# Order of the late experts in a two-layer mixture-of-experts step, and of the first products

## The reference

```python
def _hyena_filter(L, ...):                      # taps of the long convolution
    h = sin(f_freq * (feat @ f_w1 + f_b1))
    h = sin(f_freq * (h @ f_w2 + f_b2))
    return (h @ f_w3) * exp(-t * abs(decay))

def _adaln(cond, w, b):                         # w: 1024 x 6144 for each layer
    return split(silu(cond) @ w + b, 6)

def _hier_moe(x, ...):                          # for each layer
    g_sel = argmax(t @ w_group + b_group)       # one of 4 groups
    top_w, top_i = top_k(softmax(e_logits of that group), 2)
    for e in range(16):
        a, b = split(t @ w_up[e], 2)            # 1024 -> 2 x 512
        y += combine[:, e] * ((silu(a) * b) @ w_down[e])   # 512 -> 1024
```

## Time and profile before

| | us |
|---|---|
| Median of 3 runs | 1127.4 (1126.07 to 1128.08) |
| The profiled execution, its own time | 1126.63 |
| Its span in the profile | 1124.8 |
| TensorE busy | 1033.4 (92% of the span) |
| VectorE busy | 598.1 (53%) |
| ScalarE busy | 211.4 (19%) |
| GpSimd busy | 181.9 (16%) |
| Chain that ended last: TensorE | 73% of the span |
| Chain that ended last: DMA | 9% |
| Mean rate of DMA over the span | 296 GB/s |

### The profile page before, as it was taken

One profiled execution on the slowest core, in us unless ns is written; L12 is line 12 of the kernel. 1 busy time (PEld: TensorE's weight loads), 2 busy tenths in 40 slices (PEclk: granted clock), 3 DMA queues, 4 the chain that ended last, 5 costly groups with the idle time before them and its releaser, 6 DMA issues.

```text
span 1124.8 us, 26238 instructions
## 1 busy us (share of the span) xinstructions
PE 1033.4 (92%) x10516; PEld 619.3 (55%) x10516; DVE 598.1 (53%) x1404; ACT 211.4 (19%) x501; POOL 181.9 (16%) x217
## 2 busy tenths in 40 slices
PE   6999999899887999999969999999988999999773
PEld 2545555385554666666645554575455666665442
DVE  5437898745552333333389991585573333333226
ACT  4242323002310001000050000462231010000002
POOL 1200000410121222222200000254013222222112
PEclk9999999999998999999989999699989999999997
DMA  9994477940679999999987787942097998999991
GB/s 336 403 377 147 179 254 295 398 172 1 264 305 389 392 388 388 388 382 390 386 337 262 262 326 268 320 120 76 2 366 277 353 388 297 385 385 388 393 358 61
DMA packets 114954, 333.43 MB, mean 296 GB/s; under 512 B 11681, under 2 KB 24417, under 8 KB 114497
## 3 DMA queue, kind: packets, MB, share of 16 engines
q1 hardware_dynamic: 91858, 299.65, 70.4%
q0 software_dynamic: 6224, 23.05, 5.8%
q10 hardware_dynamic: 16800, 9.72, 3.1%
HBM read 323.47 MB, written 20.45 MB: 306 GB/s over the span
## 4 chain that ended last, share of the span: by engine, by line
PE 73%; DMA 9%; DVE 8%; SPq 4%; ACT 2%; issue 2%; POOL 1%; POOLq 0%; DVEq 0%; ACTq 0%
PE bank L733 71%; DMA ring<-in_moe_w_down 5%; SPq L491 3%; DMA ring<-in_moe_w_up 2%; POOL P L707 1%; PE bank L1176 1%; DVE st L1954 1%; DVE P L2012 1%; DMA bm<-in_na_bias 1%; DVE hT L1733 1%; DMA row_beta<-in_ln_b 1%; ACT x L1347 1%; DMA slots<-tok,idx_i 0%; PE bank L937 0%; DVE x L1759 0%
## 5 line engine op out<-in xcount | busy, mean ns | idle before, releaser
L733 PE MATMUL bank<-ring,xgT 128*32 128x256 f32 x4224 | 247.3, 386 | 15.2 <-DMA ring<-in_moe_w_up 14.7
L733 PE MATMUL bank<-hT,ring 128*128 128x384 f32 x640 | 207.2, 486 | 2.1 <-DVE hT L1733 2.1
L733 PEld LDWEIGHTS bank<-ring,xgT 128*32 128x32 f32 x4224 | 146.5, 111 | 97.5 <-issue 13.6
L1919 DVE TENSOR_TENSOR he<-sa,bank 128x128 f32<-128x128 f32 x66 | 19.0, 288 | 318.6 <-ACT sa L1405 318.6
L733 PEld LDWEIGHTS bank<-hT,ring 128*128 128x128 f32 x640 | 121.4, 190 | 87.5 <-issue 3.8
L685 POOL TENSOR_TENSOR yg<-ysb,gate_s 128x256 f32<-128x256 f32 x128 | 90.8, 730 | 388.6 <-ACT ysb L1410 388.6
L1555 DVE CUSTOM_DVE_ANT_0 ring<-ring,ring 128x1024 f32<-128x1024 f32 x120 | 146.9, 1224 | 4.6 <-PE bank L733 1.0
L733 PE MATMUL bank<-ring,heT 128*32 128x256 f32 x2112 | 129.7, 386 | 7.3 <-DMA ring<-in_moe_w_down 7.3
L733 PE MATMUL bank<-yg,ohT 32*128 32x256 f32 x1632 | 108.3, 394 | 2.9 <-DVE yg L1948 2.9
L733 PEld LDWEIGHTS bank<-ring,heT 128*32 128x32 f32 x2112 | 63.3, 110 | 63.2 <-issue 30.1
L733 PEld LDWEIGHTS bank<-yg,ohT 32*128 32x128 f32 x1632 | 75.3, 186 | 36.6 <-issue 27.4
(11 more groups left out here) (272 smaller groups left out, 1040.6 us busy)
## 6 DMA issues: line engine op xcount, KB each, us to landing
ring<-in_moe_w_up SPq DMA_DIRECT2D x64, 2048.0 KB, 23.7
ring<-in_moe_w_down SPq DMA_DIRECT2D x32, 2048.0 KB, 19.8
ring<-in_k_ada SPq DMA_DIRECT2D x15, 2048.0 KB, 10.3
ring<-in_w_ada SPq DMA_DIRECT2D x9, 2048.0 KB, 13.1
ring<-in_na_w_qkv SPq DMA_DIRECT2D x6, 2048.0 KB, 13.4
slots<-in_k_zero POOLq DMA_DIRECT2D x2, 5632.0 KB, 26.1
ring<-in_hy_w_in SPq DMA_DIRECT2D x5, 2048.0 KB, 12.9
group_row<-slots ACTq DMA_DIRECT2D x264, 32.0 KB, 5.2
```

The costliest lines, as they stand in the source:

```text
L733: return nc.tensor.matmul(out, lhsT, rhs, start=first, stop=last)
L1919: v.tensor_tensor(he[:], sa[:], ps[0][:, 128:256], ALU.mult).then_inc(S["he_ready"], 1)
```

## The change

Two parts.

**Order of the late experts.** The key that turns a rank into a place has a slope of 3 on one side of its top and of 1.5 on the other, where both slopes were 2 before. Rank r gets the smaller of 3r - 11.75 and -(3r - 11.75)/2, and the places go by that number: of the ranking's many end one is taken, then two of its few end. The table `MC_ORDER`, which holds the sorted keys, is changed alike.

**Beginning.** `mlp1` stands before the last two decay products. ScalarE does both sines first, then the exponentials, and its copies of modulation rows and sums are placed between them one by one. TensorE computes the rows of `cond0` before the taps, and then in turn: taps of a tile, sum of a piece, rows of the next piece. The piece pair `cond2` is now `cond2` and `cond3`; what was `cond3` to `cond7` is `cond4` to `cond8`, in the same places. VectorE copies two quarters of the decay row after each argument reduction, where it copied four after the first.

```diff
-for _name, _n in [("mlp0", 1), ("decay", 4), ("mlp1", 1), ("filt0", 4), ("cond0", 2), ("filt1", 4), ("cond1", 2), ("filt2", 4), ("cond2", 4),
-                  ("xm0", 8),
+for _name, _n in [("mlp0", 1), ("decay0", 1), ("decay1", 1), ("mlp1", 1), ("decay2", 1), ("decay3", 1),
+                  ("cond0", 1), ("filt0", 4), ("cond0_sum", 1), ("cond1", 1), ("filt1", 4), ("cond1_sum", 1),
+                  ("cond2", 1), ("filt2", 4), ("cond2_sum", 1), ("cond3", 1), ("cond3_sum", 1), ("xm0", 8),
...
+ORDER_SHIFT = 11.75
...
-    moe[:, MC_ORDER:MC_ORDER + EXPERTS] = np.arange(EXPERTS) - (EXPERTS - 0.5)
+    slope = 3.0 * np.arange(EXPERTS - FIRST) - ORDER_SHIFT
+    moe[:, MC_ORDER:MC_ORDER + EXPERTS] = np.concatenate([np.arange(FIRST) - 20.0, np.sort(np.minimum(slope, -0.5 * slope))])
...
-            for c in range(4):
-                mm(bank(G_AT["decay"] + c)[:, :], ones[:], dabs[0:1, 512 * c:512 * c + 512]).then_inc(group_ready, 1)
-            pe.wait_ge(mh_ready, 1)
-            mm(bank(G_AT["mlp1"])[:, 0:TOK], fw2, mh1[:]).then_inc(group_ready, 1)
-            pe.wait_ge(first_in, 16)
-            pe.wait_ge(scond_ready, 1)
-            pe.wait_ge(cond_sum_ready, 1)
-            pe.wait_ge(mh_ready, 2)
-            pe.wait_ge(filt_in, 32)
-            for t in range(TT):
...
-                cond(*COND_SEG[t])
+            spread_decay(0)
+            spread_decay(1)
+            pe.wait_ge(mh_ready, 1)
+            mm(bank(G_AT["mlp1"])[:, 0:TOK], fw2, mh1[:]).then_inc(group_ready, 1)
+            spread_decay(2)
+            spread_decay(3)
+            pe.wait_ge(first_in, 16)
+            pe.wait_ge(scond_ready, 1)
+            pe.wait_ge(cond_sum_ready, 1)
+            cond_rows_of(0)
+            pe.wait_ge(mh_ready, 2)
+            pe.wait_ge(filt_in, 32)
+            for t in range(TT):
+                filter_taps(t)
+                cond_sum_of(t)
+                cond_rows_of(t + 1)
+            cond_sum_of(3)
...
-            for c in range(4):
-                wait_evacuated(act, G_AT["decay"] + c)
-            decays(0)
             act.wait_ge(marg_ready, 2)
             nc.scalar.activation(mh2[:], marg[:], ACT.Sin).then_inc(mh_ready, 1)
+            for c in range(4):
+                wait_evacuated(act, G_AT[f"decay{c}"])
+            decays(0)
+            cond_rows_copied(0)
             decays(1)
-            cond(*COND_SEG[0])
+            cond_sum_copied(0)
             decays(2)
-            cond(*COND_SEG[1])
-            cond(*COND_SEG[2])
+            cond_rows_copied(1)
+            cond_sum_copied(1)
+            cond_rows_copied(2)
+            cond_sum_copied(2)
+            cond_rows_copied(3)
+            cond_sum_copied(3)
...
-                if n == 0:
-                    for c in range(4):
-                        g = G_AT["decay"] + c
-                        wait_group(dve, g)
-                        v.tensor_copy(dabs[:, 512 * c:512 * c + 512], ps[bank_of(g)][:, :]).then_inc(evacuated[g % 8], 1)
+                for c in (2 * n, 2 * n + 1):
+                    g = G_AT[f"decay{c}"]
+                    wait_group(dve, g)
+                    v.tensor_copy(dabs[:, 512 * c:512 * c + 512], ps[bank_of(g)][:, :]).then_inc(evacuated[g % 8], 1)
...
-                link(v.tensor_scalar(order_rank[:, FIRST:], order_rank[:, FIRST:], 2.0, 0.5 - late, ALU.mult, ALU.add))
+                link(v.tensor_scalar(order_rank[:, FIRST:], order_rank[:, FIRST:], 3.0, -ORDER_SHIFT, ALU.mult, ALU.add))
...
-                link(v.scalar_tensor_tensor(out=order_at[:, FIRST:], in0=order_rank[:, FIRST:], scalar=-1.0, in1=order_rank[:, FIRST:],
+                link(v.scalar_tensor_tensor(out=order_at[:, FIRST:], in0=order_rank[:, FIRST:], scalar=-0.5, in1=order_rank[:, FIRST:],
```

More of the change, by code:

```diff
@@ L106, in bank_of @@
     return (g + shift) % 8
-def ada_row(n):
-    return 0 if n == 0 else 2 * n - 1
-def ada_col(n, count):
-    return min(2 * n + 2, 2 * count - 1)
 V_ADA, V_CC, V_CS, V_BQK = 0, 96, 104, 112
@@ L439, in last_group @@
             def last_group(j):
-                for seg, _, _, count in COND_SEG:
-                    if 0 <= j - W_AT[seg] < count:
-                        return G_AT[seg] + ada_row(j - W_AT[seg])
+                for seg, _, _ in COND_SEG:
+                    if j == W_AT[seg]:
+                        return G_AT[seg]
                 for l in range(DEPTH):
@@ L541, in cond @@
             def cond(k):
-                seg, l, n0, count = COND_SEG[k]
-                for n in range(count):
-                    load(W_AT[seg] + n, A["w_ada"][l][:, (n0 + n) * 512:(n0 + n + 1) * 512], 8)
+                seg, l, n = COND_SEG[k]
+                load(W_AT[seg], A["w_ada"][l][:, n * 512:(n + 1) * 512], 8)
             def load_named(name):
@@ L584, in _ @@
                     sp.dma_start(dft[:], A["k_dft"]).then_inc(dft_in, 16)
-                    sp.wait_ge(group_ready, G_AT["decay"] + 4)
+                    sp.wait_ge(group_ready, G_AT["decay3"] + 1)
                     sp.dma_start(skip[:], bass.AP(A["hy_d"].tensor, A["hy_d"].offset, [[0, 128], [1, D]])).then_inc(dft_in, 16)
@@ L733, in mm @@
                 return nc.tensor.matmul(out, lhsT, rhs, start=first, stop=last)
-            def cond(name, l, n0, count):
-                for n in range(count + 1):
-                    if n < count:
-                        i = W_AT[name] + n
-                        out = bank(G_AT[name] + ada_row(n))
-                        wait_weights(pe, i)
-                        w = w_view(i, 8, 512)
-                        for k in range(KT):
-                            q = slice(32 * (k % 4), 32 * (k % 4) + 32)
-                            last = mm(out[q, :], scond[:, k, :], w[:, k, :], k < 4, k >= 4)
-                        last.then_inc(group_ready, 1)
-                    if n >= 1:
-                        out = bank(G_AT[name] + ada_col(n - 1, count))
-                        wait_evacuated(pe, G_AT[name] + ada_row(n - 1))
-                        for f in range(4):
-                            last = mm(out[:, 2 * f:2 * f + 2],
-                                      arow_at[l][:, (n0 + n - 1) % 2, f * 128:(f + 1) * 128], cond_sum[:])
-                        last.then_inc(group_ready, 1)
             def cond_rows_of(k):
-                name, l, n0, _ = COND_SEG[k]
+                name, l, n0 = COND_SEG[k]
                 i = W_AT[name]
@@ L896, in _ @@
                 if n in (1, 3):
[L897 removed]
+                    cond_rows_of(6 + n // 2)
                 elif n == 2:
[L899 removed]
+                    cond_sum_of(6)
                 elif n == 4:
[L901 to L903 removed]
+                    cond_sum_of(7)
+                    cond_rows_of(8)
+            cond_sum_of(8)
             pe.wait_ge(Y_ready, 3)
@@ L1325, in _ @@
                                      ).then_inc(evacuated[g % 8], 1)
-            cond_sum_copied(4)
-            for k in (5, 6, 7):
+            cond_sum_copied(5)
+            for k in (6, 7, 8):
                 cond_rows_copied(k)
```

61 lines of the change are left out of this document (23 added, 38 removed).

## The result

| | before | change |
|---|---|---|
| Median, same chip, in turn | 1125.6 us (1122.75 to 1128.08, 20 runs) | 1129.12 us (1125.59 to 1135.56, 20 runs) |
| Ratio, 95% interval | | 1.0033 (1.0020 to 1.0045) |
| The profiled execution, its own time | 1126.63 | 1125.59 |
| Its span | 1124.8 | 1123.7 |

The change makes the kernel slower by 0.33%, 3.7 us (2.3 to 5.1). The forecast was +3.0 us, "slower". One caution before the rows are read: the profiled execution of the change is the fastest of its twenty, that of before is 1 us above its median, so the two spans say the opposite of the medians. Stages and single rows are compared here, not spans.

What follows compares the result with a forecast made beforehand. TensorE and the weight stream were both taken as full in layer 0's experts, TensorE in the input projections. Beginning -4.0, layer 0 +8.1, layer 1 -1.1 gave +3.0 on 1126.6, plus 0.8 for the median: 1130.4 us, range 1125.5 to 1136.0.

Steps and rivals of the forecast that it cites:

- Layer 0, +8.1: Layer 0's experts: TensorE waits for late weight pieces at e7, e10 and e13, +8.1 us, bounds +5 and +11.
- A fall after an earlier wait is taken up by the next one: Layer 0: a clock drop after a wait before the last only shortens the next wait, as landings are fixed.
- I keep the landings: Layer 0's weight stream: slots freed earlier do not make it faster, so pieces land at their old times.
- Layer 1, -1.1: Layer 1's experts: the stream's gap at e9's down piece closes and the stage ends 1.1 us earlier, bounds -2 and +1.
- The beginning, -4.0: Before the input projections: earlier mlp1, adjacent sines and reordered TensorE work gain 4.0 us, bounds -2 and -5.
- The 0.5 us held back for VectorE's taps: Beginning: 0.5 us deducted because VectorE's taps wait on the decays, and scale and shift finish after them.
- It carries on: After the beginning: its 4.0 us gain persists, since the projections behind are TensorE work.
- The table load: ScalarE's beginning: a switch costs 1.30 us by trace, 2.66 by the skill page, which would add up to 2.7 us gain.
- A: Rival, layer 0: the stream runs ahead of the old landings, so waits don't come; 1122.3 us, chance 0.13.
- B: Rival: the beginning gives nothing, ScalarE's queue or VectorE's taps replacing the wait; 1134.4 us, or about 1132.5 with half; chance 0.15.
- C: Rival: the clock falls after layer 0's last wait and once more in layer 1; 1135 us, chance 0.12.
- D: Rival: the new key doesn't give the order it says and the old one stays; 1123.4 us, chance 0.03.

Runs made afterwards that it cites:

- begin_new_l0: begin_only with the new order of experts in layer 0 alone; 1131.07 us, ratio 1.0043 to the kernel before.
- begin_only: The change's new beginning with the old order of experts in both layers; 1120.75 us, ratio 0.9952 to the kernel before.
- begin_new_l1: begin_only with the new order of experts in layer 1 alone; 1121.5 us, ratio 0.9961 to the kernel before.
- order_only: The kernel before with the new order of experts alone, old beginning kept; 1134.87 us, ratio 1.0075 to the kernel before.
- e7: Not a run: the expert in the eighth place of a layer, counted from zero; in layer 0 one group before, five in the change.
- e10: Not a run: the expert in the eleventh place of a layer, counted from zero; in layer 0 three groups before, five in the change.
- e13: Not a run: the expert in the fourteenth place of a layer, counted from zero; in layer 0 one group before, three in the change.
- the half pieces: begin_only and the changed kernel with layer 0's weight transfers halved from e3's down piece on; layer 0 takes 227.5 us in both.
- e3: Not a run: the expert in the fourth place of a layer, counted from zero; its place is unchanged by the new order.
- e15: Not a run: the expert in the sixteenth and last place of a layer, counted from zero; in layer 0 one group before, three in the change.
- sine_late: begin_only with the second sine behind the first decay exponential, as before; 1128.68 us, ratio 1.0029 to the kernel before.
- sine_late_filled: sine_late with the rows of cond0 computed twice, filling TensorE's wait; 1122.57 us, ratio 0.9973 to the kernel before.
- mlp1_late: begin_only with mlp1 behind all four decay products and the decay row copies together, as before; 1123.3 us, ratio 0.9971 to the kernel before.
- e9: Not a run: the expert in the tenth place of a layer, counted from zero; in layer 1 one group in both orders.

## Why the prediction was right, step by step

**The forecast**: 1130.4 us, +3.0, "slower". Measured: 1129.12 us and +3.5 us by the medians. Time and reason both hold, but the closeness is in part luck: the beginning gave 5.1 us where 4.0 were forecast, the order cost 9.0 us where 8.1 - 1.1 = 7.0 were forecast, and the two misses work against each other. The forecast also stood on a median of 1127.4 for the kernel before, which over twenty runs is 1125.6.

**Layer 0, +8.1.** By the medians begin_new_l0 is 10.3 us above begin_only, and the change 7.6 above begin_new_l1, the two pairs with layer 0 alone between them; both layers together cost 8.4 (the change against begin_only) and 9.0 (order_only against before). By the stage lengths it is 7.0 (244.5 - 237.5), 6.8 (244.3 - 237.5) and 8.2 (242.6 - 234.4). The bounds were +5 and +11. From e5 on the waits came where the walk put them and nowhere else:

| | forecast | change | begin_new_l0 |
|---|---|---|---|
| e7 down | 1.6 | 2.53 | 2.42 |
| e10 up1 and down | 3.9 | 1.02 + 2.05 | 0.77 + 2.26 |
| e13 down | 2.8 | 0.59 | 2.07 |

The 0.59 at e13 is no miss of the landing. The clock fell after the wait that ends at 464.82: these down products and the next up products take 2.90 and 4.47 us where 1.93 and 3.66 are usual, 1.8 us more. The landing of e13 stood fixed, so the wait shrank by about as much, which the prediction had said ("A fall after an earlier wait is taken up by the next one"). In begin_new_l0 the wait at the same place, 2.26 us, was not followed by slow products, and e13 waits 2.07. The stretches behind the two waits, the change and then begin_new_l0 (columns as in the earlier trace rows):

```profile
464.80:472.00 7.20, 7.18 (x100) 4.71 (x104) 0.00 (x0) 0.43 (x2) 1.42 (x2) 0.76 1.03 389
...
467.10:474.30 7.20, 7.12 (x128) 4.95 (x132) 1.33 (x4) 0.66 (x2) 1.42 (x2) 1.00 1.04 390
```

"I keep the landings" is the step that carried it: against the start of e0 they moved by 0.3 and 0.6 us, and the half pieces show that nothing else is in the cost. What is fixed is the rhythm of the stream, not its distance from e0: in begin_new_l0, where e0 itself starts late, e7's down piece lands 90.1 us after e0. Counted from the down piece of e3, the first of the unbroken stream, it lands after 67.1 us in before and in the change and 67.5 in begin_new_l0, and e15's after 204.5, 203.8 and 204.1.

**Layer 1, -1.1.** The gap closed as foretold, 6.8 to 5.7 us. A gain at the end is not shown: +0.75 us in one pair of medians and -1.1 in the other, neither to be told from 0. The step that did not hold is that a gap closed in the middle of the stream reaches its end in full. The pieces behind it ran up to 1.3 us ahead, and the last one lands 237.8 us after e0 against 237.9. The 249.3 us of before against the change's 246.9 looks like a gain of 2.4, but begin_only, which has the old order, takes 246.6; 1.7 of it stand behind the last wait, 10.3 us to the close in before and 8.6 in the change, with the down products at 2.77 us instead of 1.93. The term is small and inside its bounds (-2 to +1).

**The beginning, -4.0.** Measured -5.1 by the medians (ratio 0.9952, so 3.5 to 7.3 us). In the traces the projections begin 4.3 (begin_only) and 4.7 us (the change) earlier than the 42.71 of before. The walk was 38.4; begin_only has 38.40. Both sides were to meet at 21.3, and do at 20.97; the stretch behind, 17.1 us by the rows, takes 17.08. The 0.5 us held back for VectorE's taps was the mistake: no wait for them stands in the timeline. "It carries on" holds too, though not by TensorE's work alone as the prediction has it: in begin_only e0 starts only 2.3 us earlier, and the weight stream, whose pieces for e4 end TensorE's wait 4.5 us earlier, carries the gain over that.

**The table load.** The Trainium skill, "ScalarE: Activation LUTs", section "What ACT_TABLE_LOAD costs", gives 2.66 us for a switch. The trace disagrees once more: in sine_late the load at 20.56 is followed by the sine at 21.85, 1.29 us with everything, and an estimate from the page's figure, a gain of up to 2.7 us more than the walk's, does not show in begin_only's 38.40.

**The rivals.** A (the stream runs ahead and the waits don't come): wrong, the landings keep their rhythm and moved by under 1 us. B (the beginning gives nothing): wrong, begin_only. C (the clock falls further): no fall behind the last wait of layer 0 stands in the trace of the change; one came at e10 and was taken up at e13, and behind the last wait of layer 1 there is none (8.6 us to the close). D (the old order stays): wrong, the lengths of the experts are those computed, with e7 from 405.21 and e10 from 456.37 as five-group experts.

**What stays open.** The change's 20 runs spread over 10 us (1125.6 to 1135.6), those of before over 5. Waits that sometimes drop the clock and sometimes don't, as at e10 above, could do it, but no second profile of one kernel was taken to show that. Nor is it settled why sine_late_filled gains 6.1 us with 3.2 at the projections. The two profiled executions differ by as much as the medians, 6.4 us, and their traces say where: 3.2 us at the projections, 4.6 at e0 of layer 0, 3.6 at its close, 6.5 at e0 of layer 1, 6.4 at the end. So 3 us arise between the experts of the two layers, where both kernels do the same and where the other kernels differ by as much; whether the added products have a part in it is not shown. mlp1_late loses 2.6 us by the medians with 3.8 at the projections; its profiled execution is the slowest of its twelve (1127.67 us), and with the noise of about 2 us the two don't contradict each other.

## What to carry to other kernels

Where weights come by a ring in a fixed rhythm, put long consumers where the stream would otherwise be behind and short ones where it is ahead; walk each piece's landing against its need before changing the order, since moving the same work earlier against fixed landings only turns it into waits. At the end of such a stage the last piece decides, so let a short consumer go first (its slots free the stream) and the shortest one last (least work behind the last landing): in layer 1 that was worth 10 us, while a gap of 1 us closed in the middle was worth nothing that could be measured. And test a part of a change by itself even when the whole is slower: here 5 us of gain lay under 9 us of loss.

## What the runs showed of the hardware

- A wait in the first 25 us cost more than its length. In sine_late a wait of 2.88 us was followed by 8 us of products at a granted clock of 0.57; with a repeated product in the wait's place it was 1.00, and 3.2 us came back with the awaited sine no earlier. The same 16 row products took 3.48 us in the first case (27.03) and 1.92 in the second (25.36).
- Before that the record of the clock did not tell the pace: from 15.9 to 19.5 us it says 1.00, and these 16 products take 3.64 us.
- Later in the program waits of about the same length did not always do this: 2.53 us at e7 were followed by down products of the usual 1.93 us; 2.05 us at e10 by 2.90, at a granted clock of 0.76; 2.26 us at the same place in begin_new_l0 by 1.93, at 1.00.
- Behind e3's down piece of layer 0 the one core's pieces of 2 MB landed 5.7 us apart on the mean in either order (204.5 us for 36 pieces before, 203.8 in the change), with 388 and 381 GB/s moved in all.
